# Hybrid decoder step: prompt scores in three rounded products, a sign-carrying search, and the rotary swap by transfers

## The chip, the cores and the metric

The kernel runs on one core of one Trainium2 chip. The metric is the device time in microseconds of that core; a kernel's time is the median of several executions, and one further execution is taken with the hardware profiler. TensorE multiplies matrices, VectorE (DVE), ScalarE (ACT) and GpSimd (POOL) work on rows, SyncE (SP) here only issues DMAs. They run side by side and meet at semaphores.

## The reference, cut to what matters

Two transformer layers for a prompt of 1024 tokens and 32 sample tokens (8 sequences of 4), model width 1024. Layer 0 is sparse attention, layer 1 a short convolution; both are followed by a SwiGLU. The change is in layer 0:

```
p = h @ w_in                              # 2120 columns: q (16 heads x 64), k, v (4 heads), indexer q, k, weights
q, k, qi, ki = partial_rope(...)          # the first 16 of 64 dims of a head are rotated: x1*c - x2*s, x2*c + x1*s
sc  = sum_h relu(qi_h . ki) * wi_h        # indexer score of each (query, key), -inf where not causal
sel = top_k(sc, 256)                      # 256 keys per prompt query
out = softmax(q . k over sel) @ v
```

The kernel does not gather keys. For each tile of 128 queries it finds the threshold above which 256 scores lie, makes a mask from it, and adds the mask to dense scores. Ties go to the first keys, as in the reference.

## The kernel before

All activations lie with features on partitions and tokens along the row: 1056 columns, taken as 3 chunks of 352. Numbers are float32. Large products are made of three matmuls of rounded parts (L590, `product`): high x high, high x low, low x high, where the high part is the value rounded to the short format (ScalarE copies it) and the low part the remainder (GpSimd or VectorE subtracts). Such a matmul takes one pass; a plain float32 matmul is recorded as two instructions.

**Projections.** 17 column tiles of `w_in` in the order of `ORDER`, each in 3 chunks; one (tile, chunk) is an item. Tiles 0 to 4 (indexer, `pe_proj_a`, L930) come before the indexer, tiles 5 to 16 (k, v, q, `pe_proj_b`, L961) after it. ScalarE evicts an item from PSUM (`act_evac_rope`, L997). For the rotation, TensorE multiplies the evicted item by a constant 128 x 128 matrix `rotm` that swaps rows 0-7 with 8-15 of each head (`pe_rot`, L844). In the first part VectorE multiplies the result with the sines and adds the cosine part (`dve_rope`, L1085); in the second ScalarE evicts it to `pafB` (`act_rot`, L1008) and GpSimd multiplies and adds (`pool_fin`, L1109). The cosine part is GpSimd's (`pool_cos`, L1102). Rotated q goes through DRAM (`q_scr`) and comes back to `hhi` after the last product (`sp_att`, L1389). Between items TensorE also multiplies chunks of the conditioning matrix (`pe_chunks`, L851), whose weights SyncE loads.

**Indexer and search.** `pe_index`, `act_index` and `dve_index` make the scores of query tiles 2 to 7 in `s_all`. Then VectorE searches the thresholds bit by bit (`dve_select`, L1578) while TensorE works on tiles 5 to 16: 32 rounds, in each of which VectorE counts the scores of tiles 2 to 5 and the samples against a candidate, and ScalarE those of tiles 7 and 6 (`act_count`, L893), at places in its own order that `count_halves` (L101) writes down in advance. The scores of a tile are first multiplied by a sign, so that all thresholds are positive, and multiplied back when the masks are made.

**Attention.** 64 pairs (`NPAIR`), pair n being query tile n // 8 and head step n % 8, two heads at once in two groups of 64 partitions. The order of a pair on each engine, with four slots of probabilities and scores three pairs ahead (`pe_att`, L1915):

- TensorE: turns (transposes) of the first head's probabilities (L1866, L1871), values of pair n-1 (L1884), turns of the second head's, scores of pair n+3 (`pe_scores`, L1838; plain float32, L1855), chunks of the conditioning matrix.
- VectorE: a step or two of the masks (`dve_masks_at`, L1713, pairs 0 to 27), evictions of turns, the inverse of the sums of pair n+1 (L1949), the output of pair n-1, mask and minimum of pair n+3 (L1942).
- ScalarE: eviction of each head's turn (L1993), exponential of pair n+2 (L1986), output of pair n-1 (L1998); then splits of output weights in pairs 49, 52, 55 and 58.
- GpSimd: normalisation of pair n by the inverse (L2023), which TensorE's turn of pair n waits for; then the low parts of output weights in pairs 50, 53, 56 and 59.

Query tiles 0 and 1 have fewer than 256 keys and take the causal mask alone.

Of the kernel before, what the change touches and what calls it, by code (L numbers as in the profile page):

```python
# [350 lines left out]
def program(nc, x_prompt, x_sample, c_prompt, c_sample, cache_k, cache_v, cache_kidx, state_conv, page_table,  # L351
            ada_w, ada_b, norm1_g, norm2_g, final_g, attn_w_in, attn_w_out, conv_w_in, conv_k, conv_w_out,
            ffn_w_gu, ffn_w_down, k_ident, k_rot, k_cos, k_sin, k_causal, k_causal_s, k_bitf, k_biti,
# [10 lines left out]
    with ExitStack() as ctx:  # L364
# [22 lines left out]
        (rotm,) = place(616 + 540, ("rotm", [P, P], F32))  # L387
# [94 lines left out]
        def wide(i):  # L482
# [15 lines left out]
        evac, rot_mm, ts_rdy, pm_rdy, qc_rdy, fin_rdy = (sem(x) for x in (  # L498
            "evac", "rot_mm", "ts_rdy", "pm_rdy", "qc_rdy", "fin_rdy"))
# [125 lines left out]
        def sp_start(sp):  # L625
# [22 lines left out]
            sp.dma_start(rotm[:], k_rot).then_inc(const_loaded, 16)  # L648
# [31 lines left out]
        def dve_start(dve):  # L680
            dve.memset(ones[:], 1.0)
            dve.memset(bv[:, 0:9], 1.0).then_inc(f_st, 1)
# [158 lines left out]
        def rot_bank(r):  # L841
            return bank[(3, 5)[r % 2] if r < 15 else (3, 4)[r % 2]]
# [50 lines left out]
        def act_count(act, half):  # L893

            for h in range(64):
# [34 lines left out]
        def pe_proj_a(pe):  # L930
            pe.wait_ge(const_loaded, 64)
            pe.wait_ge(ada_read, G0)
            for p in range(5):
                for n in range(NCH):
# [3 lines left out]
                    for r in {0: (), 1: (), 2: (0,), 3: (1, 2)}.get(3 * p + n, (3 * p + n - 1,)):  # L938
                        pe_rot(pe, r)
# [10 lines left out]
            pe_rot(pe, 14)  # L950
# [10 lines left out]
        def pe_proj_b(pe):  # L961
            pe.wait_ge(relu_rdy, 8 * len(TILES))
            for n in range(NCH):
                pe_tile(pe, 5, n)
                if n:
                    pe_rot(pe, R_AT[5] + n - 1)
                pe_chunks(pe, ITEM_AT[5] + n)
            pe.wait_ge(up_lo, 8)
            for tt in range(9):
# [7 lines left out]
                if tt == 0:  # L977
                    pe_rot(pe, R_AT[5] + 2)
                pe_chunks(pe, ITEM_AT[6] + tt)
            for p in (8, 9):  # L980
                for n in range(NCH):
                    pe_tile(pe, p, n)
                    if p == 9 or n:
                        pe_rot(pe, R_AT[p] + n - 1)
                    pe_chunks(pe, ITEM_AT[p] + n)
            pe.wait_ge(fin_rdy, R_AT[9])
            for p in range(10, 17):
                for n in range(NCH):
                    pe_tile(pe, p, n)
                    pe_rot(pe, R_AT[p] + n - 1)  # L990
# [3 lines left out]
            pe_rot(pe, R_AT[16] + 2)  # L994
            pe_ada_turned(pe, SG_W - 1)

        def act_evac_rope(act, p, n, dst):  # L997
# [3 lines left out]
            after(act, rot_mm, r - 1)  # L1001
# [6 lines left out]
        def act_rot(act, r):  # L1008

            act.wait_ge(rot_mm, r + 1)  # L1010
            after(act, fin_rdy, r - 1)
            act.activation(pafB[:, r % 2, :], rot_bank(r)[:, 0:CH], ACT.Copy).then_inc(ts_rdy, 1)

        def act_proj_a(act):
            for p in range(5):
                for n in range(NCH):
                    if p or n:
                        act_evac_rope(act, p, n, psgA)
                proj_hi(act, p + WR)
# [8 lines left out]
        def act_proj_b(act):  # L1028
            for n in range(NCH):
                act_evac_rope(act, 5, n, psgB)  # L1030
                act_count(act, 2 * (ITEM_AT[5] + n))
                if n:
                    act_rot(act, R_AT[5] + n - 1)
                act_chunks(act, ITEM_AT[5] + n)
            for tt in range(9):
# [5 lines left out]
                if tt == 0:  # L1041
                    act_rot(act, R_AT[5] + 2)
                    proj_hi(act, 9)
                act_chunks(act, ITEM_AT[6] + tt)
            for p in (8, 9):
                for n in range(NCH):
                    act_evac_rope(act, p, n, psgB)
                    act_count(act, 2 * (ITEM_AT[p] + n))
                    if p == 9 or n:
                        act_rot(act, R_AT[p] + n - 1)  # L1050
# [4 lines left out]
            for p in range(10, 17):  # L1055
                for n in range(NCH):
                    act_evac_rope(act, p, n, psgB)
                    act_count(act, 2 * (ITEM_AT[p] + n))
                    act_rot(act, R_AT[p] + n - 1)
# [5 lines left out]
            act_rot(act, R_AT[16] + 2)  # L1065
# [19 lines left out]
        def dve_rope(dve, r):  # L1085
# [3 lines left out]
            dve.wait_ge(rot_mm, r + 1)  # L1089
            after(dve, fin_rdy, r - 1)  # L1090
            dve.tensor_tensor(pafA[0:rows, r % 2, :], rot_bank(r)[0:rows, 0:CH], ropeS[0:rows, chunk(n)], ALU.mult)\
# [17 lines left out]
        def pool_fin(pool, r):  # L1109

            p, n = (5, r - 15) if r < 18 else (8 + (r - 18) // 3, r % 3)
            pool.wait_ge(ts_rdy, r + 1)
            pool.tensor_tensor(pafB[:, r % 2, :], pafB[:, r % 2, :], ropeS[:, chunk(n)], ALU.mult).then_inc(pm_rdy, 1)
            pool.wait_ge(pm_rdy, r - 14)
# [12 lines left out]
        def pool_proj_b(pool):  # L1127
            for p in (5,) + tuple(range(8, 17)):
# [2489 lines left out]
```

## Time and profile before

| | |
|---|---|
| time, median of 3 runs | 2634.79 us (2630.44 to 2640.76) |
| profiled execution | 2635.32 us, span of the profile 2633.5 us |
| TensorE, matmul | 2512.0 us busy, 95% |
| VectorE, ScalarE, GpSimd | 1771.3, 1101.9, 1287.4 us busy |
| granted TensorE clock | 0.983 of full speed, mean |

The span is the time from the first to the last instruction; the few microseconds around it belong to the execution's own time. Busy times are sums over instructions. PE stands for TensorE's matmuls, PEld for its weight loads, and SPq for SyncE's queue. L12 is line 12 of the kernel. A busy TensorE is not one at its peak, since matmuls are pipelined.

### The profile page before, as it was taken

The numbers are of one execution on the slowest core, as the hardware profiler recorded it, in microseconds if no ns is written. First come the engines' busy times: TensorE is split into PE (matmuls) and PEld (weight loads), VectorE is DVE, ScalarE is ACT, GpSimd is POOL, SyncE is SP. The second block draws the span as 40 slices with busy tenths as digits, with TensorE's granted clock in tenths as the row PEclk, the third lists the DMA queues.
The fourth block names the chain that finished last, engine by engine and source line by source line (L and its number), as shares of the span: only waits on it lengthen the run. The fifth ranks groups of instructions, "written<-read, shape, count | busy, mean of one in ns | idle before, by whom it ended". The sixth has DMA issues, their size and how long they took to land.

```text
span 2633.5 us, 51699 instructions
## 1 busy us (share of the span) xinstructions
PE 2512.0 (95%) x20164; PEld 2312.3 (88%) x20164; DVE 1771.3 (67%) x3137; ACT 1101.9 (42%) x2061; POOL 1287.4 (49%) x967
## 2 busy tenths in 40 slices
PE   6979999999998999999999989999989999999999
PEld 4848874677798999999999989999989999999999
DVE  6388888665347756656567687767785665656775
ACT  5155656775235444344212343332454444442223
POOL 3404652344134656566544545545455656654454
PEclk7999999999999999999999999999999999999999
DMA  9205557201433435344894333328334534469731
GB/s 322 78 21 153 177 207 255 70 2 68 129 113 101 146 124 164 117 155 139 328 349 167 117 98 106 107 82 328 117 98 131 164 117 155 139 207 366 278 131 70
DMA packets 316390, 408.00 MB, mean 155 GB/s; under 512 B 40816, under 2 KB 227032, under 8 KB 313338
## 3 DMA queue, kind: packets, MB, share of 16 engines
q1 hardware_dynamic: 316154, 404.75, 45.9%
q8 instruction: 161, 2.64, 0.4%
q14 instruction: 75, 0.61, 0.1%
HBM read 284.85 MB, written 119.85 MB: 154 GB/s over the span
## 4 chain that ended last, share of the span: by engine, by line
PE 70%; DVE 11%; DMA 6%; issue 5%; POOL 4%; ACT 2%; SPq 2%; ACTq 0%; DVEq 0%; POOLq 0%
PE PS L595 10%; PE PS L2492 9%; PE PS L2494 9%; PE PS L2493 9%; PE PS L2553 5%; PE PS L2555 5%; PE PS L2556 5%; PE PS L1855 3%; PE PS L1884 2%; PE PS L1866 2%; POOL ring L2864 2%; DMA t_scratch<-stage 2%; DMA a_scratch<-stage 1%; POOL stage L2877 1%; DVE s_all L1552 1%
## 5 line engine op out<-in xcount | busy, mean ns | idle before, releaser
L2492 PE MATMUL PS<-th,ring 128*128 128x264 f32 x2800 | 800.2, 286 | 19.9 <-DVE y L3007 8.2
L2494 PE MATMUL PS<-th,ring 128*128 128x264 f32 x2800 | 796.8, 285 | 0.0
L2493 PE MATMUL PS<-th,ring 128*128 128x264 f32 x2800 | 795.9, 284 | 0.0
L2492 PEld LDWEIGHTS PS<-th,ring 128*128 128x128 f32 x2800 | 527.8, 189 | 26.8 <-issue 26.1
L2493 PEld LDWEIGHTS PS<-th,ring 128*128 128x128 f32 x2800 | 528.0, 189 | 0.0
L2494 PEld LDWEIGHTS PS<-th,ring 128*128 128x128 f32 x2800 | 527.9, 189 | 0.0
L2864 POOL TENSOR_TENSOR ring<-wraw,ring 128x512 fp32r<-128x512 f32 x232 | 340.3, 1469 | 368.1 <-ACT ring L2648 367.8
L2864 POOL TENSOR_TENSOR ring<-sums,ring 128x512 fp32r<-128x512 f32 x216 | 322.2, 1493 | 276.3 <-ACT ring L2648 276.3
L2553 PE MATMUL PS<-th,ring 128*128 128x264 f32 x1232 | 354.8, 288 | 14.3 <-DVE zs L3196 6.7
L2555 PE MATMUL PS<-th,ring 128*128 128x264 f32 x1232 | 352.9, 286 | 0.0
L2556 PE MATMUL PS<-th,ring 128*128 128x264 f32 x1232 | 352.5, 286 | 0.0
L2648 ACT ACTIVATE ring<-wraw 128x512 fp32r<-128x512 f32 x340 | 211.8, 626 | 299.2 <-PE PS L2556 168.2
L3193 DVE SCALAR_TENSOR_TENSOR y<-PS,mod,y 128x528 f32<-128x528 f32 x308 | 235.0, 766 | 141.2 <-PE PS L2556 128.0
L3007 DVE TENSOR_TENSOR y<-y,PS 128x528 f32<-128x528 f32 x150 | 104.9, 699 | 293.8 <-PE PS L2494 293.6
L2648 ACT ACTIVATE ring<-sums 128x512 fp32r<-128x512 f32 x216 | 136.1, 631 | 353.2 <-PE PS L2494 173.3
L2553 PEld LDWEIGHTS PS<-th,ring 128*128 128x128 f32 x1232 | 234.4, 190 | 16.1 <-issue 11.7
L2556 PEld LDWEIGHTS PS<-th,ring 128*128 128x128 f32 x1232 | 234.7, 191 | 0.0
L2555 PEld LDWEIGHTS PS<-th,ring 128*128 128x128 f32 x1232 | 234.6, 190 | 0.0
L2877 POOL TENSOR_TENSOR stage<-y,stage 128x528 fp32r<-128x528 f32 x110 | 179.2, 1629 | 77.3 <-ACT stage L2668 77.3
L595 PE MATMUL PS<-hhi,uhi 128*128 128x352 f32 (+1 forms) x552 | 189.0, 342 | 14.5 <-DVE hlo L1267 7.3
L2696 ACT ACTIVATE y<-PS 128x528 f32<-128x528 f32 x173 | 105.1, 607 | 186.4 <-PE PS L2494 185.3
L595 PE MATMUL PS<-hhi,ulo 128*128 128x352 f32 (+1 forms) x552 | 180.8, 328 | 0.0
(393 smaller groups left out, 5164.4 us busy)
## 6 DMA issues: line engine op xcount, KB each, us to landing
t_scratch<-stage SPq DMA_DIRECT2D x154, 528.0 KB, 3.3
th<-t_scratch SPq DMA_DIRECT2D x77, 1056.0 KB, 8.7
wraw<-in_ffn_w_gu_dram SPq DMA_DIRECT2D x96, 512.0 KB, 5.2
wraw<-in_ada_w_dram SPq DMA_DIRECT2D x80, 512.0 KB, 4.8
wraw<-in_ffn_w_down_dram SPq DMA_DIRECT2D x80, 256.0 KB, 5.9
wraw<-in_conv_w_in_dram SPq DMA_DIRECT2D x28, 512.0 KB, 5.3
y<-y_scratch SPq DMA_DIRECT2D x12, 1056.0 KB, 8.9
y_scratch<-y SPq DMA_DIRECT2D x6, 2112.0 KB, 7.9
```

What stands on the lines that cost most here:

```text
L595: last = pe.matmul(out, w(kt), x(kt), start=(n == 0), stop=(n == 3 * count - 1))
L2492: pe.matmul(out, hi, x[:, TH, k, :], start=(k == 0 and i in (1, 2, 5)), stop=False, skip_group_check=True)
L2493: pe.matmul(out, hi, x[:, TL, k, :], start=False, stop=False, skip_group_check=True)
L2494: last = pe.matmul(out, lo, x[:, TH, k, :], start=False, stop=(k == 3), skip_group_check=True)
L2553: pe.matmul(out, hi, x[:, TH, 2 * k + s, :], start=(k == 0 and i in (1, 2, 5)), stop=False, skip_group_check=True)
L2555: pe.matmul(out, hi, x[:, TL, 2 * k + s, :], start=False, stop=False, skip_group_check=True)
L2556: last = pe.matmul(out, lo, x[:, TH, 2 * k + s, :], start=False, stop=(k == 1), skip_group_check=True)
L2648: act.activation(slot_of(p)[:, RH, :], split_source(p), ACT.Copy).then_inc(w_hi, 1)
L2696: act.activation(out, result(r, it.groups), ACT.Silu if it.kind == "g" and pos == 6 else ACT.Copy).then_inc(rd_a, 1)
L2864: pool.tensor_tensor(w[:, RL, :], split_source(p), w[:, RH, :].bitcast(F32), ALU.subtract).then_inc(w_lop, 1)
L2877: pool.tensor_tensor(lo.rearrange("p (s n) -> p s n", s=2), token_part(v, i), hi.rearrange("p (s n) -> p s n", s=2), ALU.subtract).then_in ...
L3193: ins = dve.scalar_tensor_tensor(out=out, in0=result(r, BOTH), scalar=gate_of(f, m)[:, 0:1], in1=out, op0=ALU.mult, op1=ALU.add)
```

## The change

1. **Rotation.** `rotm`, `pe_rot` and `act_rot` are gone. ScalarE issues DMAs that copy rows 8-15 of each head onto rows 0-7 of a second buffer and the other way round (`act_swap`, from the evicted item, four transfers of 8 rows by 352 columns, two for the three items of tile 0). The rest of that buffer is zeroed once. VectorE and GpSimd wait for the transfers.
2. **Search.** Scores are no longer multiplied by a sign. The candidate carries it, and bits are set with exclusive or; 31 rounds in place of 32; the five small steps of a round stand behind all counts. `count_halves` spaces ScalarE's counts anew.
3. **Masks** lose their multiplication by the sign.
4. **Scores of tiles 2 to 7.** q comes back to `hlo`. ScalarE writes rounded halves of q and k (`act_q_hi`), GpSimd the remainders (`pool_q_lo`), k in pairs 0 to 4, q in pairs 5 to 27, and TensorE makes three matmuls for each of the old ones. Tile 4 is cut in 320 + 320 columns. The halves of k hold two of the four slots of split weights to the last scores.
5. **Output weights** are split in pairs 50, 61, 62 and 63, on ScalarE and GpSimd in the same pair.

```diff
-    return [next(s for s, t in enumerate(at) if t >= 24 + 4.9 * h) for h in range(64)]
+    return [next(s for s, t in enumerate(at) if t >= 14 + 5.2 * h) for h in range(62)]
...
-        def pe_rot(pe, r):
-            rows = P if r >= 3 else 64
-            pe.wait_ge(evac, rope_m(r) + 1)
-            after(pe, ts_rdy, r - 1)
-            src = (psgA if r < 15 else psgB)[0:rows, r % 2, :]
-            pe.matmul(rot_bank(r)[0:rows, 0:CH], rotm[0:rows, 0:rows], src, start=True, stop=True).then_inc(rot_mm, 1)
+        def swap_done(eng, r):
+
+            if r >= 0:
+                eng.wait_ge(swapped[r % 2], sum(32 if x < 3 else 64 for x in range(r % 2, r + 1, 2)))
+
+        def act_swap(act, r):
+
+            act.wait_ge(evac, rope_m(r) + 1)
+            after(act, fin_rdy, r - 1)
+            if r in (15, 16):
+                act.wait_ge(pm_rdy, 1)
+            src, dst = (psgA, pafA) if r < 15 else (psgB, pafB)
+            for head in (0,) if r < 3 else (0, 64):
+                for o in (head, head + 8):
+                    of = 2 * head + 8 - o
+                    act.dma_start(dst[o:o + 8, r % 2, :], src[of:of + 8, r % 2, :]).then_inc(swapped[r % 2], 16)
...
                     act_evac_rope(act, p, n, psgB)
                     act_count(act, 2 * (ITEM_AT[p] + n))
-                    act_rot(act, R_AT[p] + n - 1)
+                    act_swap(act, R_AT[p] + n)
...
-            dve.tensor_tensor(pafA[0:rows, r % 2, :], rot_bank(r)[0:rows, 0:CH], ropeS[0:rows, chunk(n)], ALU.mult)\
+            swap_done(dve, r)
+            dve.tensor_tensor(pafA[0:rows, r % 2, :], pafA[0:rows, r % 2, :], ropeS[0:rows, chunk(n)], ALU.mult)\
...
-            return xn[:, t, at] if t == KT - 1 else hhi[:, t, at].bitcast(F32)
+            return xn[:, t, at] if t == KT - 1 else hlo[:, t, at].bitcast(F32)
+
+        SPLIT0 = 2
+        K_AT, KL_AT = {0: 0, 1: 1}, {1: (0, 0), 2: (0, 1), 3: (1, 0), 4: (1, 1)}
+        Q_AT = {5: (2, 0), 7: (2, 1), 9: (3, 0), 11: (3, 1)} | {13 + 2 * x: (4 + x // 2, x % 2) for x in range(8)}
...
+        def act_q_hi(act, n):
+
+            if n in K_AT:
+                a = K_AT[n]
+                act.wait_ge(up_mm, UP_END[14 + a])
+                act.wait_ge(fin_rdy, 21)
+                act.activation(k_part(uhi, a), kT[:, a, 0:SEQ], ACT.Copy).then_inc(q_hi, 1)
+            if n in Q_AT:
...
+                ts = slice(4, KT - 1) if h else slice(0, 4)
+                ins = act.activation(hhi[:, ts, at], hlo[:, ts, at].bitcast(F32), ACT.Copy)
+                if h:
+                    act.wait_ge(fin_rdy, 45)
+                    ins = act.activation(hlo[:, KT - 1, at], xn[:, KT - 1, at], ACT.Copy)
+                ins.then_inc(q_hi, 1)
+
+        def pool_q_lo(pool, n):
...
+            if n in Q_AT:
+                i, h = Q_AT[n]
+                at = slice(P * i, P * i + P)
+                pool.wait_ge(q_hi, Q0 + 2 + 2 * (i - SPLIT0) + h + 1)
+                ts = slice(4, KT - 1) if h else slice(0, 4)
+                ins = pool.tensor_tensor(hlo[:, ts, at], hlo[:, ts, at].bitcast(F32), hhi[:, ts, at].bitcast(F32), ALU.subtract)
+                if h:
+                    ins = pool.tensor_tensor(hhi[:, KT - 1, at], xn[:, KT - 1, at], hlo[:, KT - 1, at].bitcast(F32), ALU.subtract)
+                ins.then_inc(q_lo, 1)
...
+            with dve.Fori(0, ROUNDS) as i:
+                dve.wait_ge(sel, i * 6 + base)
+                count(2, None, ALU.is_ge)
+                dve.wait_ge(cand_rdy, i + 1)
+                signal(count(6, None, ALU.is_lt))
+                count(3, None, ALU.is_ge)
+                count(4, None, ALU.is_ge)
+                signal(count(5, None, ALU.is_ge))
+                dve.wait_ge(sel, i * 6 + (base + 1))
                 dve.wait_ge(sign_cnt, i * NA + NA)
...
+                signal(dve.tensor_tensor(v(lt, 0, 3), v(cnt, 0, 3), v(kk, 0, 3), ALU.is_gt))
...
             if step == 0:
-                link(dve, dve.tensor_scalar(s, s, bv[0:rows, BS + 3 * E + j:BS + 3 * E + j + 1], None, ALU.mult))
                 link(dve, dve.tensor_scalar(A, s, t, 0.0, ALU.is_gt, ALU.add, accum_out=n))
...
+            if i < SPLIT0:
...
+            if t % 4 == 0:
+                pe.wait_ge(q_lo, Q0 + 4 + 2 * (i - SPLIT0) + t // 4 + 1)
+            (hi, lo), a = q_parts(i, t), t // 4
+            cs = pieces(i)
             for j, c in enumerate(cs):
-                for g in range(2):
-                    last = pe.matmul(wide(2 * g)[:, c], q_of(i, t)[64 * g:64 * g + 64],
-                                     kT[64 * g:64 * g + 64, t // 4, c], start=True, stop=True)
-                    if j == len(cs) - 1:
-                        last.then_inc(s_mm, 1)
+                for x, (q, w) in enumerate(((hi, uhi), (lo, uhi), (hi, ulo))):
+                    for g in range(2):
+                        last = pe.matmul(score_of(i, g, j, c), q[64 * g:64 * g + 64], k_part(w, a)[64 * g:64 * g + 64, c],
+                                         start=(x == 0), stop=(x == 2))
+                        if j == len(cs) - 1 and x == 2:
+                            last.then_inc(s_mm, 1)
...
                 act_pair_chunks(act, n)
-                if n in (49, 52, 55, 58):
-                    split_hi(act, "out", (n - 49) // 3, MM0["out"])
+                act_q_hi(act, n)
+                if n in OUT_AT:
+                    if n > 60:
+                        act.wait_ge(s_mm, 2 * NPAIR)
+                    split_hi(act, "out", OUT_AT.index(n), MM0["out"])
...
                     pool.tensor_scalar(p, p, bv[:, at:at + 1], 1.0, ALU.mult, ALU.mult).then_inc(p_nrm, 1)
-                if n in (50, 53, 56, 59):
-                    split_lo(pool, "out", (n - 50) // 3)
+                pool_q_lo(pool, n)
+                if n in OUT_AT:
+                    split_lo(pool, "out", OUT_AT.index(n))
```

## Rows read from the trace of the kernel before

**Rows 1.** The page, part 1: busy us of each engine (share of span), instructions.
```profile
PE 2512.0 (95%) x20164; PEld 2312.3 (88%) x20164; DVE 1771.3 (67%) x3137; ACT 1101.9 (42%) x2061; POOL 1287.4 (49%) x967
```

**Rows 2.** Windows by stage: stretch, length, busy us, clock, DMA share, GB/s.
```profile
65.00:134.00 69.00, 65.97 (x372) 58.53 (x372) 27.70 (x57) 12.40 (x23) 33.24 (x28) 0.95 0.29 79
...
185.00:382.00 197.00, 194.29 (x1342) 162.34 (x1343) 175.86 (x636) 111.91 (x223) 101.33 (x95) 0.98 0.51 157
...
382.00:482.00 100.00, 90.35 (x829) 45.78 (x828) 80.20 (x248) 62.16 (x215) 32.04 (x62) 0.95 0.78 254
...
386.00:397.00 11.00, 9.15 (x58) 3.84 (x58) 5.31 (x24) 3.86 (x20) 2.96 (x8) 0.53 0.94 350
```

**Rows 3.** Chain of waits from 262 us: start, us, engine, line.
```profile
264.28 4.01 PE PS L595 x24
...
268.30 0.59 PE PS L849 x2
```

**Rows 4.** The same view, 382 to 652 us, shares by line.
```profile
by line: PE PS L1855 24.7%; PE PS L1884 24.0%; PE PS L1866 20.8%; DMA wraw<-in_ada_w_dram 8.2%; PE PS L1871 5.8%; PE PS L1897 4.6%; issue 3.1%; DVE mscr L1699 2.3%; DVE PbS L1942 1.3%; DVE mscr L1697 0.8%; POOL PbS L2023 0.8%; DVE s_all L16
```

**Rows 5.** Groups by line, ScalarE, 185-382 us: busy, mean ns, idle before.
```profile
L900 ACT ACTIVATE junkA<-s_all,bv 128x1024 bf16<-128x1024 f32 x64 | 69.8, 1091 | 41.0 <-DVE bv L1640 41.0
...
L1005 ACT ACTIVATE psgB<-PS 128x352 f32<-128x352 f32 x30 | 13.8, 460 | 35.9 <-PE PS L595 35.9
```

**Rows 6.** Timeline, SyncE's queue: start us, us of issuing, line.
```profile
4.58 0.30 SPq L635 DMA_DIRECT2D vst<-in_c_prompt_dram  x1
...
4.92 0.66 SPq L636 DMA_DIRECT2D vst<-in_c_sample_dram  x1
```

**Rows 7.** DMA issues: count, KB each, median us to landing.
```profile
q_scratch<-qst_ SPq DMA_DIRECT2D x21, 176.0 KB, 2.5
```

**Rows 8.** Timeline, pair 5: start us, us, engine, line, idle before.
```profile
404.13 0.30 PE L1866 MATMUL PS<-ident,PbS 128*128 128x128 f32 x1
...
404.64 0.39 ACT L1986 ACTIVATE PbS<-PbS,bv 128x128 f32<-128x128 f32 x1
...
405.53 0.72 POOL L2023 TENSOR_SCALAR PbS<-PbS,bv 128x128 f32<-128x128 f32 x2 [3.14 <-DVE bv L1949]
...
406.00 0.33 PE L1866 MATMUL PS<-ident,PbS 128*128 128x128 f32 x1
```

**Rows 9.** Timeline, pair 27.
```profile
479.59 0.66 PE L1866 MATMUL PS<-ident,PbS 128*128 128x128 f32 x4
...
480.78 0.71 ACT L1986 ACTIVATE PbS<-PbS,bv 128x512 f32<-128x512 f32 x1
...
481.54 0.66 PE L1866 MATMUL PS<-ident,PbS 128*128 128x128 f32 x4
```

**Rows 10.** Timeline, pair 50.
```profile
576.65 0.66 PE L1866 MATMUL PS<-ident,Pb 128*128 128x128 f32 x4
...
579.27 0.66 PE L1866 MATMUL PS<-ident,Pb 128*128 128x128 f32 x4
```

**Rows 11.** Timeline, pair 61.
```profile
637.97 0.66 PE L1866 MATMUL PS<-ident,Pb 128*128 128x128 f32 x4
...
638.30 2.21 POOL L2023 TENSOR_SCALAR Pb<-Pb,bv 128x1024 f32<-128x1024 f32 x2 [3.65 <-DVE bv L1949]
...
639.16 1.14 ACT L1986 ACTIVATE Pb<-Pb,bv 128x1024 f32<-128x1024 f32 x1
...
639.47 0.66 PE L1866 MATMUL PS<-ident,Pb 128*128 128x128 f32 x4 [0.41 <-POOL Pb L2023]
```

**Rows 12.** The page, part 5: remainder and rounded half, 512 columns.
```profile
L2864 POOL TENSOR_TENSOR ring<-wraw,ring 128x512 fp32r<-128x512 f32 x232 | 340.3, 1469 | 368.1 <-ACT ring L2648 367.8
...
L2648 ACT ACTIVATE ring<-wraw 128x512 fp32r<-128x512 f32 x340 | 211.8, 626 | 299.2 <-PE PS L2556 168.2
```

**Rows 13.** Lines 580 and 587, the same of 1024 columns: ns min/median/max.
```profile
L580 ACT ACTIVATE uhi<-wraw x12: 1039/1053/1062, 573.7 to 782.6; 128x1024 fp32r<-128x1024 f32 x12
...
L587 POOL TENSOR_TENSOR ulo<-wraw,uhi x12: 2362/2373/2422, 574.8 to 783.7; 128x1024 fp32r<-128x1024 f32 x12
```

More of the change, by code:

```diff
@@ L681, in dve_start @@
             dve.memset(ones[:], 1.0)
+            dve.memset(pafA[:], 0.0)
             dve.memset(bv[:, 0:9], 1.0).then_inc(f_st, 1)
@@ L893, in act_count @@
         def act_count(act, half):
-            for h in range(64):
+            for h in range(62):
                 if COUNT_AT[h] == half:
@@ L1592, in dve_select, with v, vi @@
-            one = lambda r, j: v(r, j, j + 1)
-            ka = bank[5][:, 432:432 + NA]
-            groups = ((0, NA), (NA, E))
-            def count(j, threshold):
+            cnt, lt, kk, low, th, cand, inc = range(7)
+            held = {lt: 384, kk: 400, inc: 416}
+            tiny = 1.1754943508222875e-38
+            def v(r, a=0, b=E):
+                return bank[5][:, held[r] + a:held[r] + b] if r in held else bv[:, BS + E * r + a:BS + E * r + b]
+            def vi(r, a=0, b=E):
+                return v(r, a, b).bitcast(I32)
@@ L1598, in count, with one @@
+            def one(r, j):
+                return v(r, COL[j], COL[j] + 1)
+            def count(j, threshold, op):
                 s, rows, L, _ = entries[j]
                 at = threshold if isinstance(threshold, float) else one(cand, j)[0:rows]
-                return dve.tensor_scalar(junk(j, rows, L), s, at, 0.0, ALU.is_ge, ALU.add,
-                                         accum_out=one(cnt, j)[0:rows])
+                return dve.tensor_scalar(junk(j, rows, L), s, at, 0.0, op, ALU.add, accum_out=one(cnt, j)[0:rows])
@@ L1603, in dve_select, with signal @@
+            def signal(ins):
+                ins.then_inc(sel, 1)
             dve.wait_ge(smp_rdy, 1)
             dve.wait_ge(score_rdy, 8 * len(TILES))
-            link(dve, dve.memset(bv[:, BS:BS + 7 * E], 0.0))
+            link(dve, dve.memset(v(cnt), 0.0))
             for j in range(E):
-                ins = count(j, 0.0)
+                ins = count(j, 0.0, ALU.is_ge)
+            for j in range(NA):
+                dve.memset(one(kk, j), float(entries[j][2] - 2 * entries[j][3]))
+            dve.memset(one(kk, E - 1), float(entries[E - 1][2] - entries[E - 1][3]))
@@ L1608, in dve_select @@
             link(dve, ins)
[L1609 to L1610 removed]
+            for a, b, k in ((0, 2, KP), (2, 3, KS), (3, E, KP)):
+                dve.tensor_scalar(v(th, a, b), v(cnt, a, b), float(k), 2.0, ALU.is_ge, ALU.mult)
+                ins = dve.tensor_scalar(v(cand, a, b), v(cnt, a, b), float(k), -1.9999998807907104, ALU.is_lt, ALU.mult)
             link(dve, ins)
[L1613 to L1615 removed]
@@ L1616, in dve_select @@
-            link(dve, ins)
-            for j, (s, rows, L, k) in enumerate(entries):
-                if j < NA:
-                    dve.tensor_scalar(ka[:, j:j + 1], one(kk, j), -2.0, float(L), ALU.mult, ALU.add)
-                dve.tensor_scalar(s, s, one(sig, j)[0:rows], None, ALU.mult)
-            ins = dve.memset(v(cand), 2.0)
+            ins = dve.tensor_tensor(v(cand), v(cand), v(th), ALU.add)
             link(dve, ins)
@@ new lines, in dve_select @@
+            nsel[0] += 6 * ROUNDS
+            dve.wait_ge(sel, nsel[0])
+            dve.wait_ge(cand_rdy, ROUNDS + 1)
+            dve.scalar_tensor_tensor(out=v(inc, 0, NA), in0=v(cand, 0, NA), scalar=tiny, in1=v(cand, 0, NA),
+                                     op0=ALU.is_ge, op1=ALU.mult)
+            link(dve, dve.tensor_scalar(v(lt, 0, NA), v(cand, 0, NA), 0.0, -tiny, ALU.is_lt, ALU.mult))
+            link(dve, dve.tensor_tensor(v(low, 0, NA), v(cand, 0, NA), v(lt, 0, NA), ALU.min))
+            link(dve, dve.tensor_tensor(v(th, 0, NA), v(inc, 0, NA), v(low, 0, NA), ALU.add))
@@ L1825, in program @@
         LA = NSLOT - 1
+        OUT_AT = (50, 61, 62, 63)
         def mask_of(i):
@@ L3568, in _constants @@
         S[o:o + 8], S[o + 8:o + 16] = -sin, sin
-        for d in range(8):
-            R[o + 8 + d, o + d] = R[o + d, o + 8 + d] = 1.0
     q, x = np.arange(P)[:, None], np.arange(SEQ)[None, :] - (SEQ - P)
```

172 lines of the change are left out of this document (70 added, 102 removed).

## The prediction

> **What bounds the kernel now.** I read the page first: TensorE is busy for 95% of the span [rows 1], so time leaves this kernel mostly where TensorE gets less to do or waits less. The windows by stage then say where the change falls [rows 2]: projections up to the indexer (65 to 134 us), the indexer, projections beside the search (185 to 382), attention pairs (382 to 652). Everything after 652 us, three quarters of the span, keeps its code; it only starts earlier or later. In both projection stretches TensorE is busy for nearly all of the time (65.97 of 69 and 194.29 of 197 us). The chain of waits there is nothing but its lines: a product of 24 matmuls of 352 columns in 4.01 us, then two passes of the rotation matmul, L849, in 0.59 us [rows 3]. In the attention stretch the chain of waits is scores (L1855), values (L1884) and turns (L1866) of TensorE, 70% together, with 8.2% of transfers [rows 4]. The last view is the timeline of single pairs, where I followed who frees whom: TensorE turns the probabilities, ScalarE evicts and exponentiates, GpSimd normalises the next pair, TensorE turns that one.
>
> **The rotation as transfers.** Removed: 45 matmuls of 0.59 us, 15 before the indexer and 30 after it [rows 3]. They lie on the chain, so 8.8 and 17.7 us of TensorE go. Added on ScalarE's queue are four transfers of 8 rows for each of them (two for the first three), 174 in all. Issuing is not shown for ScalarE. SyncE's small ones took 0.30 and 0.66 us [rows 6]; I take 0.33, so 1.3 us for a swap of four, as the 8-row one is the nearest. Zero is the lower end, where issuing runs beside an activation already handed over. ScalarE's load for an item of the second stretch is then: eviction 0.46 us; counts, 64 of 1.09 us with a read behind them over 39 items, some 2.1 us [rows 5]; weight splits, 8 of 1.05 us [rows 13], turned keys and the like some 0.5 together, an estimate; swaps 1.3; the eviction of the rotated rows goes. That is 4.4 us against TensorE's item of 5.2 - 0.6 = 4.6 us. It just fits; ScalarE waits 41.0 us for the search and 35.9 us for TensorE there now [rows 5], and that is the cover. With 0.66 us an issue it is 5.7 us an item and the cover is gone (a rival below). Landing: 176 KB take 2.5 us from issue [rows 7]; I take 2.5 for the small ones, bounds 1 and 6. A swap has one whole item before its buffer is wanted, so this costs nothing, except at two ends. Before the indexer the last swap takes 1.3 + 2.5 us where the matmul took 0.59; about half of the difference lies beside VectorE's additions for the item before, so +1.5. Before attention TensorE's third pair waits for the last rotated rows behind the same chain, in a stretch where DMA is at its limit (share 0.94 [rows 2]): +3. Sum: 8.8 - 1.5 = -7 before the indexer; -16 beside the search (17.7 less 10% for hold-ups by the shared order of evictions and counts); +3 at the start of attention. Together -20 us, bounds -27 and 0.
>
> The nearest row is of 176 KB and 128 partitions, and shows only that a transfer is not free of a fixed part. By the Trainium skill (DMA: Bandwidth & Descriptors, Rules for kernel authors) many small transfers should be joined, since below 64 KB one pays mostly overhead; no row here has 11 KB in one transfer. The Trainium skill gives 2.0 us as the fixed part of a transfer (same page, Anatomy of one DMA, measured there on GpSimd's path); with 2.0 in place of 2.5 us of landing the sum would be the same within a microsecond.
>
> **The search with signs carried.** One round less, one multiplication of each score tile less in front, two chains of three small steps made into one. ScalarE waits 41.0 us for the search [rows 5] and TensorE, busy for 194.29 of 197 us, waits for neither [rows 2]: the rounds run at TensorE's pace. With less to do in each and one fewer, I take it that they can follow the shorter item too, and cost them at nothing; the cover is TensorE's 4.6 us item. Without it each round would add its excess 31 times, up to the whole 16 us of the stretch. The masks lose one instruction of seven. They stand on the chain with L1699 and L1697, 3.1% of 270 us [rows 4]; I count nothing, bound -1.
>
> **Scores in three products.** The chain holds L1855 for 24.7% of 270 us, 66.7 us [rows 4], for 36,864 key columns in all pairs, 1.85 us per 1024. Now 1024 columns are six matmuls of 512 for each of two row groups. By [rows 3] a rounded matmul of 352 columns takes 0.167 us, so one of 512 at most 0.243, and six 1.46, if the two row groups run beside each other as they do in the four-pass form. That saves 0.39 us per 1024, over the 33,792 columns of tiles 2 to 7 12.9 us. Pairs in which TensorE waits anyway (below) give nothing back: -10, bounds -15 and 0. That the groups don't overlap is a rival.
>
> **The splits, and who waits for them.** This is the step I find dear. ScalarE makes the rounded half of q at the *end* of its work for pair n (`act_q_hi`), and GpSimd takes the remainder after the normalisation of the same pair n (`pool_q_lo`). GpSimd executes in order, so the normalisation of pair n+1, for which TensorE's next turn waits, stands behind a wait for ScalarE's end of pair n and the subtraction. Count from the second turn of pair n. Pair 5 [rows 8]: turn at 404.13, last exponential over at 405.03 (+0.90); rounded half 0.63, remainder 1.47 for 512 columns [rows 12]; first half of a normalisation 0.36. That makes +3.4 with a wait or two; the next turn now comes at +1.87. Price 1.6 us. Pair 27 [rows 9]: exponential and its read over at +1.90, rounded half and remainder in two pieces each 0.8 and 1.6, half a normalisation 0.7: +5.0, now +1.95. Price 3.0. There are 12 such pairs, every second from 5 to 27; between these ends, less at three of them where a transfer is late already, I read 22 us. Even pairs, where VectorE's masks and transfers hold TensorE a little now, give 2 back: +20, bounds +10 and +28. The splits of k are one pair or more apart and hold nobody.
>
> The output weights' splits have the same form now (`OUT_AT`: both engines in the same pair), where before GpSimd came one pair later. Pair 61 [rows 11]: exponential over at 640.30 + the read, +2.4 from the turn at 637.97; rounded half 1.05 and remainder 2.37 [rows 13], half a normalisation 1.1: +6.9, now +1.5. Price 5.4. Pair 62 has no exponential any more: 1.3 + 1.05 + 2.37 + 1.1 = +5.8 against some 1.4: 4.4. Pair 50 [rows 10]: 2.3 + 1.05 + 2.37 + 1.0 = +6.7 against +2.62: 4.1. The one of pair 63 is followed by no turn. Sum +14, bounds +10 and +16. TensorE idles for 4 to 5 us there. Its granted clock fell to 0.53 (the lower level, 1.2 GHz, for nearly all of it) in 386 to 397 us, after a stretch with short bursts [rows 2]; I add 2 us, bounds 0 and 8.
>
> **Sum.** -20 (swaps) + 0 (search) - 10 (scores) + 20 + 14 (waits for splits) + 2 (clock) = +6. The profiled execution took 2635.3 us (span 2633.5), half a microsecond above the median of 2634.8: forecast **2641 us**.
>
> **Rivals.**
> 1. *The splits are hidden* (2607 us). GpSimd is busy for a third of the attention stretch [rows 2], and three pairs of slots stand between scores and turn. If the wait for ScalarE cost GpSimd only its idle time, the terms +20, +14 and +2 go and 2635 - 20 - 10 = 2605 to 2609 remains. For it: GpSimd idles 3.1 to 3.7 us before its normalisations [rows 8, 11]. Against it: it idles because VectorE's inverse is late, and the order of the code puts the whole of ScalarE's pair in front.
> 2. *ScalarE becomes the bound beside the search* (2661). From 0.45 us an issue upwards its item is 4.9 us or more, from 0.55 on no gain of the 16 is left, and the same evictions reach GpSimd late: 2641 + 16 + 4. For it: 0.66 in [rows 6]; against it: the 8-row transfer's 0.30, and issuing may run beside counts.
> 3. *The row groups of a rounded matmul don't run beside each other* (2684). Twice 1.46 us per 1024 columns against 1.85: +1.07 x 33 = +35 in place of -10, some of it in pairs that wait anyway. Nothing in the trace has this form; the four-pass form overlaps.
> 4. *The clock stays low through the pairs with splits* (2655): each pair of pairs then has 2 to 3 us of idle. For it: 0.53 in 386 to 397 us, at the start of attention; against it: 0.95 over the whole of 382 to 482 us, which has gaps of 1 to 2 us too [rows 2]. From 10 us at the lower level on it decides.
>
> **How the numbers follow.** A change below 0.5% (13 us) can't be told from none here. My forecast has 0.45 (of it 0.80 within 13 us, 0.15 beyond it slower, 0.05 faster); rival 1 0.25 (0.9 faster); rival 2 0.15 (0.8 slower); rival 3 0.07 (slower); rival 4 0.08 (0.65 slower). So faster 0.25, same 0.44, slower 0.31. The range 2606 to 2668 takes in rival 1 and rival 2 and leaves out rival 3; the likeliest case by itself has 2629 to 2655.
>
> **What would show it.** Each step has its place in the profile after: no L849 and items of 4.6 us beside the search; the start of attention some 20 us earlier; in every second pair from 5 to 27 an idle of TensorE of 1.5 to 3 us released by GpSimd's normalisation, and GpSimd waiting for `act_q_hi`; idles of 4 to 5 us at pairs 51, 62 and 63; scores of 1024 columns in 1.5 us. Wrong it would be if ScalarE's queue shows issues above 0.45 us and TensorE waits for evictions, if GpSimd's normalisations come as early as now, or if two score matmuls of different row groups stand one behind the other.

## The result, and the profile after

| | before | after |
|---|---|---|
| median, us | 2635.2 | 2679.9 (2679.3 to 2683.8) |
| ratio to before | 1 | 1.0177, 95% interval 1.0163 to 1.0191 |
| profiled execution: span, us | 2633.5 | 2678.3 |

Slower by 45 us (1.8%), outside the range 2606 to 2668. The median before is that of four executions, the three of the table further up and one more. The page's busy times hardly moved: TensorE is busy for 6 us less than in [rows 1], at a lower mean granted clock (0.967 against 0.983), so the loss is waiting and a slower clock.

```profile
PE 2505.6 (94%) x20234; PEld 2329.1 (87%) x20234; DVE 1764.1 (66%) x3001; ACT 1101.4 (41%) x2047; POOL 1313.5 (49%) x990
```

To find the place I read the start times of the same events in both traces and subtracted them ("lag": after minus before, us; period sums are from pair to pair).

| event | before | after | lag |
|---|---|---|---|
| last eviction of a projection before the indexer | 126.0 | 121.0 | -5.0 |
| first one behind the indexer | 192.6 | 191.4 | -1.2 |
| last one beside the search | 379.9 | 364.9 | -15.0 |
| first turn of attention | 387.6 | 377.2 | -10.4 |
| turn of pair 5 | 403.3 | 392.2 | -11.1 |
| turn of pair 29 | 484.8 | 516.5 | +31.7 |
| turn of pair 50 | 574.1 | 600.9 | +26.8 |
| turn of pair 52 | 584.5 | 617.7 | +33.2 |
| turn of pair 61 | 635.1 | 665.3 | +30.2 |
| turn of pair 63 | 643.8 | 686.4 | +42.6 |
| end | 2633.5 | 2678.3 | +44.8 |

Two jumps make the loss: pairs 5 to 28 (+42.8) and the four pairs 50, 51, 61 and 62 (+18.7). All the rest together is a gain of 16.7 us, though the lag also grows in two places ahead of attention: by 3.8 us across the indexer, and by 4.6 us between the last eviction beside the search and the first turn. Single executions differ there: in six kernels with the same projections, swaps and search (this one, `no_scores`, `q_lag`, `both_lag`, `spread_lag` and `padded`, below) it starts between 375.1 and 378.1 us.

Windows of the changed kernel, against [rows 2] (length, then busy us of PE, PEld, DVE, ACT, POOL, granted clock, DMA share, GB/s). Read the clock column: 0.82 where it was 0.95.

```profile
65.00:134.00 69.00, 58.97 (x348) 54.12 (x346) 36.16 (x59) 14.20 (x25) 33.61 (x28) 0.90 0.35 93
...
382.00:482.00 100.00, 78.31 (x656) 41.41 (x654) 61.71 (x175) 50.71 (x176) 39.84 (x60) 0.82 0.55 180
```

The same view with one window a pair, pairs 21 to 24. In the odd ones, where q is split, TensorE is busy for 3.3 of 6.7 us; in the even ones it is busy from end to end, but at half the clock (1.2 GHz at 0.50) for much or nearly all of it, and takes 5.4 and 6.4 us for what took 4.1 before.

```profile
468.90:475.58 6.68, 3.30 (x37) 1.89 (x33) 6.27 (x10) 3.13 (x9) 2.85 (x3) 1.00 0.73 236
475.58:481.02 5.44, 5.44 (x42) 3.46 (x43) 1.46 (x4) 2.66 (x7) 1.63 (x3) 0.69 0.01 2
481.02:486.97 5.95, 3.25 (x34) 1.85 (x32) 4.52 (x13) 3.21 (x10) 2.13 (x4) 0.91 0.65 211
486.97:493.40 6.43, 6.43 (x43) 3.93 (x43) 1.46 (x4) 2.88 (x7) 1.96 (x3) 0.55 0.18 50
```

The chain of waits through pair 25 (start, us, engine and line) shows what TensorE idles for. After a last turn at 495.07 it is ScalarE's eviction (L2037), its exponential with the read of its sum (L2030), its rounded half of q (L1406), GpSimd's remainder (L1425), GpSimd's normalisation (L2070), and only then the next turn (L1908) at 500.03: 4.4 us, one behind the other.

```profile
495.07 0.60 PE PS L1908 x4
495.68 0.02 issue
495.70 0.03 ACT PT L2037
...
496.19 0.81 ACT PbS L2030 x2
497.00 0.53 ACT hhi L1406
497.53 0.07 issue
497.60 1.27 POOL hlo L1425
498.87 1.12 POOL PbS L2070
499.99 0.04 issue
500.03 1.11 PE PS L1908 x4
```

Issues of the swap's transfers on ScalarE's queue in the stretch beside the search (count, ns min/median/max). The median is nearly twice the assumed 0.33 us. 52 of the 120 run in part beside an instruction that ScalarE had been handed before them, most often a count, so issuing does run beside other work: from the first to the last eviction of this stretch (191.4 to 364.9 us) ScalarE executes for 96.8 us and issues for 74.0, 27 of them at the same time, and has nothing to do for 30.

```profile
L855 ACTq DMA_DIRECT2D pafB<-psgB x120: 631/632/1205, 191.9 to 368.0; - x120
```

Timeline of TensorE in pair 41: the three products of a score tile. x2 is the two row groups. The products start 0.33, 0.24 and 0.22 us after one another for both groups together, where the prediction took 0.243 for one matmul of 512 columns, so the groups run beside each other.

```profile
559.22 0.50 PE L1897 MATMUL PS<-uhi,hhi 64*128 64x512 f32 x2
559.55 0.39 PE L1897 MATMUL PS<-uhi,hlo 64*128 64x512 f32 x2
559.79 0.39 PE L1897 MATMUL PS<-ulo,hhi 64*128 64x512 f32 x2
560.01 0.28 PE L1897 MATMUL PS<-uhi,hhi 64*128 64x256 f32 x2
```

### The profile page after: what moved, and what is told of

It is laid out like the page before. It is cut to its first block, busy times and chain, and to the rows that moved or that the text cites. A ratio compares the mean times of both kernels' runs of the same rounds, so it can differ in the third digit from the quotient of the medians.

```text
span 2678.3 us, 51888 instructions
## 1 busy us (share of the span) xinstructions
PE 2505.6 (94%) x20234; PEld 2329.1 (87%) x20234; DVE 1764.1 (66%) x3001; ACT 1101.4 (41%) x2047; POOL 1313.5 (49%) x990
## 4 chain that ended last, share of the span: by engine, by line
PE 65%; DVE 11%; issue 6%; POOL 6%; DMA 5%; ACT 4%; ACTq 2%; SPq 1%; DVEq 0%; POOLq 0%
PE PS L2540 9%; PE PS L2542 9%; PE PS L2541 9%; PE PS L2601 4%; PE PS L594 4%; PE PS L2603 4%; PE PS L2604 4%; PE PS L1926 3%; PE PS L1908 3%; PE PS L1897 2%; POOL ring L2912 2%; ACTq L855 1%; DMA a_scratch<-stage 1%; DVE s_all L1603 1%; PE PS L2562 1%
## 5 line engine op out<-in xcount | busy, mean ns | idle before, releaser
L594 PE MATMUL PS<-hhi,uhi 128*128 128x352 f32 (+1 forms) x552 | 187.3, 339 | 14.6 <-DVE hlo L1257 7.3
L594 PE MATMUL PS<-hhi,ulo 128*128 128x352 f32 (+1 forms) x552 | 180.9, 328 | 0.0
```

What stands on the lines that cost most here:

```text
L594: last = pe.matmul(out, w(kt), x(kt), start=(n == 0), stop=(n == 3 * count - 1))
```

## The experiments

All medians in us; each ratio is against the kernel before, run on the same chip beside it. "Turn n" is the start of the first turn of pair n in the profiled execution.

### The parts alone

Three kernels carry one part of the diff each, on the kernel before.

`scores_only` (products, `act_q_hi`, `pool_q_lo`, `OUT_AT`):

> The kernel before with the attention's part of the change alone: prompt scores in three products of rounded halves, with the rounding of keys, queries and output weights where the changed kernel has it; rotation by TensorE and the old search stay. Theory A (the loss is made inside the attention, by VectorE's and TensorE's wait for the halves): the first turn to the last took 256.2 us before and 309.2 us after, so this kernel shows nearly all of it, +50 to +56 us (about 2688 us), more than the whole change, because the transfers' gain is missing. Rival B (ScalarE's issues of transfers are what costs): this kernel is at most +25 us (2660 us).

Measured 2689.1 (four executions, 2679.9 to 2695.5), ratio 1.019 (1.0155 to 1.0224): +55. First to last turn 312.4 us against 256.2. Theory A; the attention's part alone costs more than the whole change.

`swap_only`:

> The kernel before with the rotary swap by transfers alone. Theory A: faster by about 10 us (2625 us), since the first turn of the attention came 10.4 us earlier in the changed kernel. Rival B: each issue holds ScalarE 0.63 us where 0.33 us was assumed, ScalarE then holds back the search and the projections, and the kernel is slower by 10 us or more (2645 us). Rival C: the earlier start came from the new search, and the swaps alone change nothing beyond 3 us.

Measured 2635.8, ratio 0.9999 (0.9988 to 1.001): nothing. A's 10 us are missing; the first turn came 3.7 us earlier (383.9), and pairs 0 to 4 took 18.3 us instead of 15.7. That was the clock: TensorE was busy for 17.9 of the 18.3 us, all of it at the lower level (granted clock 0.50 from 367 to 408 us), where before it is back at 1.00 from pair 3 on. Rival B fails too: ScalarE was not what held it. By line in 185 to 382 us (busy, mean ns, idle before, releaser), its counts waited 41.6 us for VectorE's search.

```profile
L906 ACT ACTIVATE junkA<-s_all,bv 128x1024 bf16<-128x1024 f32 x64 | 69.8, 1090 | 46.1 <-DVE bv L1630 41.6 <-issue 4.5
```

The chain of waits had been TensorE's products there [rows 3]. In `swap_only` it is the search on VectorE (L1590 to L1635) and the short gaps between its steps ("issue"); the products (L594) are down to 7.7%. From the first to the last eviction beside the search it took 182.8 us, 187.3 before and 173.6 to 176.8 where the new search is there too.

```profile
by line: issue 32.5%; DVE junkA L1590 10.6%; PE PS L594 7.7%; DVE junkC L1590 7.4%; ACTq L855 6.6%; DVE PS L1628 4.6%; ACT junkA L906 4.3%; DVE junkB L1590 4.2%; DMA wraw<-in_ada_w_dram 2.6%; DVE bv L1630 2.5%; DVE bv L1635 2.3%; DVE PS L16
```

`search_only`:

> The kernel before with the sign-carrying search alone (31 rounds instead of 32, one step less in each mask, other places for ScalarE's counts). Theory A: within 4 us of before (2631 to 2639 us), as the projections set the pace beside the search. Rival C: it brings the 10 us that the attention starts earlier (2625 us).

Measured 2635.5, ratio 1.0 (0.9986 to 1.0013). Theory A.

`no_scores` has both of these parts together:

> The changed kernel with the attention of before: swaps by transfers and the new search, plain scores. Theory A (swap alone and search alone gave nothing, since each time the other held the pace, and together they start the attention 10 us earlier): about 2625 us, 8 to 12 us faster than before. Rival E (the earlier start is lost again in the attention's first pairs, on the weight transfers that pace them): 2632 us or more. With the version that has both low halves later, its difference tells what the three products are worth without waits: 6 to 9 us by theory A.

Measured 2624.7, ratio 0.996 (0.9948 to 0.9973): 10.4 us faster (the profiled execution, 2634.7, is the slowest of six). Neither part is worth anything alone, and together they give 10: the new search lets VectorE follow the shorter item. Rival E is out.

### The wait

`q_lag`, one edit to the changed kernel:

```
-                pool_q_lo(pool, n)
+                if n:
+                    pool_q_lo(pool, n - 1)
```

> The changed kernel with one edit: GpSimd takes the low half of keys and queries one pair later, behind the normalising of the next pair, so that it finds ScalarE's rounding done; the same instructions, the same number. Theory A (the loss of pairs 5 to 28, 43 us, is GpSimd's wait behind ScalarE's rounding, and TensorE's clock that falls in the pair behind each such wait): most of the 43 us go, 30 to 40 us, to about 2643 us, and the granted clock between 392 and 516 us goes from about 0.8 to over 0.95. Rival D (GpSimd's 1.2 us for the low half itself, not the wait, is too long for a pair): at most 15 us go (2665 us or more).

Measured 2633.7, ratio 1.0002 (0.9985 to 1.0018): 46 us back, more than theory A said. Pairs 5 to 28 took 79.3 us (before 81.5, after 124.3) with the same instructions. The window from 382 to 482 us has the clock at its upper level (2.4 GHz) throughout, and GpSimd busy for 55 of 100 us:

```profile
382.00:482.00 100.00, 95.07 (x982) 56.67 (x971) 81.91 (x238) 77.34 (x246) 55.30 (x83) 1.00 0.67 216
```

Rival D is out: GpSimd has time for its remainders; what cost was that it waited for ScalarE's last work of the pair with a normalisation queued behind.

`both_lag` keeps that edit and does the same with the output weights:

```
-                if n in OUT_AT:
-                    split_lo(pool, "out", OUT_AT.index(n))
+                if n - 1 in OUT_AT:
+                    split_lo(pool, "out", OUT_AT.index(n - 1))
+            split_lo(pool, "out", 3)      # behind the loop
```

> The changed kernel with both low halves one pair later on GpSimd: those of keys and queries, as in the run before, and those of the four output weights (behind the normalising of pairs 51, 62, 63, the last behind pair 63). Theory A (what is left of the attention's loss is the same wait at pairs 50, 61 and 62): pairs 50 and 51 together and 61 and 62 together go from 15.8 and 20.6 us to about 10.5 and 11 us, so 12 to 16 us below the version with the queries alone, about 2619 us, faster than before. Rival D (GpSimd's 2.34 us for one output weight is itself too long for a pair of 4.4 us): at most 5 us (2629 us).

Measured 2617.5, ratio 0.9927 (0.9899 to 0.9954), faster than before. Pairs 50 and 51 took 9.87 us together (15.83 with the queries alone), 61 and 62 also 9.87 (20.58). Rival D is out here too. By the medians it is 7.2 us faster than `no_scores`, which is about what the three products are worth without waits (6 to 9 were expected; the two intervals overlap a little, from 0.9948 to 0.9954).

`spread_lag` is `both_lag` without its last line, and moves the rounding to pairs 50, 59, 61, 62:

```
-        OUT_AT = (50, 61, 62, 63)
+        OUT_AT = (50, 59, 61, 62)
-                    if n > 60:
-                        act.wait_ge(s_mm, 2 * NPAIR)
+                    if n > 58:
+                        act.wait_ge(s_mm, 2 * NPAIR if n > 60 else 120)
```

> Both low halves one pair later, and the output weights' rounding spread to pairs 50, 59, 61 and 62 (low halves in 51, 60, 62, 63), since the first weight's and the last one's slots hold no key halves. Theory A: pairs 61 and 62 together take 8.8 to 9.0 us instead of 9.9, so 1 us off, 2616 us; it stays 16 to 19 us faster than before. Rival H (the half in pair 60 now collides with the full work of that pair, or the product behind the attention doesn't depend on it at all): no gain, 2617 to 2620 us.

Measured 2615.1, ratio 0.9939 (0.9924 to 0.9954). The intervals of the two overlap and pairs 61 and 62 still took 9.87 us, so theory A's microsecond is not there. The chain in `both_lag` shows why: the rounded half made at the end of pair 61 (L579) is still late for GpSimd in pair 62 (L586). `spread_lag` has the same pieces in the same place, 0.95 us at 618.47 and 2.35 us at 619.50, for another weight.

```profile
622.96 1.23 ACT Pb L2030 x2
624.19 0.95 ACT uhi L579
625.14 0.07 issue
625.22 2.35 POOL ulo L586
627.57 1.11 POOL Pb L2070
```

### The clock

`padded` is the changed kernel with its waits kept and filled: TensorE turns the identity 14 times ahead of the waits of pairs 6, 8, ... 28.

```
+            if g == 0 and n in range(6, 30, 2):
+                after(pe, eva, turned(n, g) - 1)
+                for j in range(14):
+                    pe.transpose(bank[4][:, 0:P], ident[:], ident[:])
             pe.wait_ge(p_nrm, turned(n, g))
```

> The changed kernel with GpSimd's wait as it is, but TensorE turns the identity 14 times (about 2.1 us of idle time filled, into the bank that the next turning writes) ahead of each even pair from 6 to 28. Theory A (the even pairs are longer only because the clock falls behind the wait of the odd pair): the 16 us that the even pairs grew by shrink to less than 5 us and the even pairs run at a granted clock over 0.9; the odd pairs stay as they are; some 8 to 14 us faster than the changed kernel, about 2669 us. Rival F (even pairs wait on the halves too): no gain, or slower by what the turnings cost, 2680 us or more.

Measured 2658.5, ratio 1.0094 (1.0074 to 1.0114): 21 us faster than the changed kernel with more work in it, more than expected. In the profiled executions 17.8 us of it lie in pairs 5 to 28; the rest lies where the edit is not, 2.1 of it ahead of the first turn. Its pairs 21 and 22:

```profile
456.97:463.66 6.69, 4.99 (x51) 3.41 (x47) 6.24 (x13) 3.13 (x9) 2.86 (x3) 1.00 0.74 235
463.66:467.60 3.94, 3.94 (x43) 2.43 (x44) 1.47 (x4) 2.48 (x7) 1.63 (x3) 1.00 0.02 4
```

The odd pair is as long as in the changed kernel (6.69 us), the even one is 3.94 instead of 5.44. Sums over the twelve of each:

| us | before | after | padded | queries later |
|---|---|---|---|---|
| odd pairs 5 to 27 | 42.5 | 69.5 | 68.7 | 40.8 |
| even pairs 6 to 28 | 38.9 | 54.8 | 37.8 | 38.5 |

So of the loss in pairs 5 to 28, 27 us are waiting and 17 us are the clock (the even pairs would otherwise have got 1.1 us shorter). In ten of the twelve even pairs the clock fell close to the end of the wait, between 1.1 us before and 1.8 us behind it, and was low in the pair that followed. The other two even pairs, 8 and 14, ran at 1.00, and only they did not grow: 2.54 and 3.07 us, against 2.54 and 3.19 before. The Trainium skill has this for waits on DMA (TensorE: Matmul & The Clock Gate, HAM oscillation: a wait in every step makes each step start at the slow clock); the runs agree, with an engine as the one waited for.

### The price of a transfer's issue

`half_swap` leaves out the swap of the second head of each pair of heads (on `both_lag`), two issues instead of four:

> The version with both low halves later, with two transfers a swap instead of four (the second head of each pair is left unrotated: part of the computation left out). Theory A (an issue holds ScalarE 0.63 us, and this bounds the projections beside the search as much as its work does): 27 projections lose 1.3 us of ScalarE each, and the first turn comes 10 to 25 us earlier, about 2605 us. Rival G (products, the search on VectorE or GpSimd's rotation hold the pace, the issues only fill ScalarE's idle time): the first turn within 4 us, 2615 us or more.

Measured 2609.2, ratio 0.9904 (0.9883 to 0.9925), an interval that overlaps that of `both_lag`; first turn at 370.3 against 378.1. That is 8 us, or 5 to 8 against the six kernels with the same projections and four issues: between the two theories, and not where theory A put it. From the first to the last eviction beside the search it took 173.8 us, no less than the six with four issues (173.6 to 176.8). The gain lies at the ends: 67.3 us across the indexer (last eviction before it to first one behind it) against 68.5 to 70.9, and 10.4 us from the last eviction to the first turn against 12.1 to 12.8.

`split_swap` cuts each transfer into halves of the columns (on `both_lag`), eight issues:

```
-                    act.dma_start(dst[o:o + 8, r % 2, :], ...)
+                    for part in (slice(0, 176), slice(176, 352)):
+                        act.dma_start(dst[o:o + 8, r % 2, part], ...)
```

> The version with both low halves later, each of the four transfers of a swap cut into two of half the columns: eight issues of 0.63 us, 2.6 us more of ScalarE's time for each swap. Theory A (an issue is as dear for half the bytes, and ScalarE's issues share in setting the pace beside the search): 27 projections get longer by up to 2.6 us, the first turn comes 25 to 60 us later, at 403 us or more, and the kernel is slower than before (2645 to 2680 us). Rival G (ScalarE has idle time for them): the first turn at most 10 us later (2628 us or less).

Measured 2719.3, ratio 1.0322 (1.0305 to 1.0339): first turn at 477.0, 99 us later. Its issues still took 0.63 us each, at half the bytes; 174 more of them are 110 us of ScalarE, and 90% of that shows. A part of the 99 us is the clock, which was not separated: it was granted 0.90 over 185 to 382 us, against 0.96 in `both_lag`. The shares of the chain of waits in 230 to 350 us with two, four and eight issues:

```profile
by line: PE PS L594 80.0%; PE PS L868 11.3%; DMA wraw<-in_ada_w_dram 4.4%; PE PS L961 1.6%; SPq L806 0.8%; SPq L745 0.6%; PE PS L881 0.5%; ACT psgB L1000 0.4%; SPq L744 0.4%; issue 0.2%
```

```profile
by line: issue 21.0%; ACTq L855 19.7%; PE PS L594 15.3%; ACT junkA L906 14.7%; DVE junkA L1654 5.3%; DMA wraw<-in_ada_w_dram 4.4%; ACT psgB L1000 3.4%; DVE junkC L1654 2.2%; PE PS L868 2.0%; DVE PS L1691 1.3%; ACT ktok L1016 1.3%; ACT uhi L
```

```profile
by line: ACTq L856 39.0%; PE PS L594 16.7%; issue 15.5%; ACT junkA L907 11.7%; PE PS L869 3.3%; DMA wraw<-in_ada_w_dram 3.2%; ACT psgB L1001 2.2%; POOL ulo L833 2.0%; POOL pafB L1101 1.6%; ACT uhi L827 1.2%; POOL kT L1107 1.0%; ACT ktok L10
```

With two issues the products hold the pace; with four the chain of waits passes between TensorE, ScalarE and its issues, which costs at most 3 us by the times above, so ScalarE's queue is near balance; with eight ScalarE holds the pace (246.7 us beside the search). There theory A holds, and by more than it said.

`no_swap_both_lag` puts TensorE's rotation back:

> Rotation by TensorE as before, new search, three products with both low halves one pair later. Theory A (the swaps bring their 10 us once the new search lets VectorE keep pace): slower by 8 to 12 us than the version with the swaps, about 2627 us, first turn at 387 to 390 us. Rival I (the swaps are worth nothing here either): within 3 us of it, 2615 to 2621 us.

Measured 2627.0, ratio 0.9974 (0.9961 to 0.9987), first turn at 383.4. With the new search and the later halves in place the swaps are worth 9.5 us by the medians. The profiled executions alone show less, 5.3 us at the first turn and 4.9 at the end; they differ by several us from one execution of a kernel to the next. Rival I is out; the first turn came 4 us earlier than expected.

## Why the prediction was wrong

Measured 44.8 us of span against +6 forecast, 39 more. Of these 21 lie in pairs 5 to 28 (+42.8 against +20 and the clock's +2), 10 in the swaps, 5 in the output weights, and the rest in what the scores gave less and behind the last turn.

**The step that failed: the clock behind the waits for splits.** The waits were predicted as they are, line for line: exponentials, rounded half, remainder, half a normalisation, turn. The term for the clock, "I add 2 us, bounds 0 and 8", was mis-sized: it is 17 us in pairs 6 to 28, and some 5 more in pairs 51 and 62.
- *Even pairs.* The sum took +20 for pairs 5 to 28, by "Even pairs [...] give 2 back". They took 15.9 us more instead. `padded` shows that this is the clock.
- *Odd pairs.* Prices of 1.6 and 3.0 us were worked out for pairs 5 and 27; 2.1 and 2.9 were measured. Their mean over twelve pairs is 27.6 us, but the prediction took 22; the twelve make 27.0 (0.76 to 2.9 each).
- *The clock.* Rival 4 had it at 10 us and more, with a chance of 0.08. The argument against it, 0.95 over 382 to 482 us with gaps of 1 to 2 us in it [rows 2], read gaps shorter than the predicted waits would add (TensorE idled 3.4 us in pair 21 and 2.7 us in pair 23). The row that applied was the 0.53 of 386 to 397 us: in the 5.6 us before the first turn of the kernel before, from 382.00 to 387.61, TensorE was busy for 1.9.

**Output weights**: +14 predicted; 5.4, 4.4 and 4.1 us for pairs 61, 62 and 50. Measured +5.4, +6.9 and +4.1, and +2.2 in pair 51 behind it: 18.7. The waits of pairs 61 and 50 are right. What is over, 2.5 us in pair 62 and 2.2 in pair 51, is put down to the clock by its level there (0.65 and 0.64); no run fills these waits.

**Swaps**: -20 predicted, -10.4 at the first turn, with the new search (9.5 by `no_swap_both_lag`). The three parts:
- *Before the indexer*, -7 predicted, -1.2 measured at the first eviction behind it. This is the larger part of the miss. The prediction gave issues and landing a price only for the last swap, since "A swap has one whole item before its buffer is wanted, so this costs nothing, except at two ends". Landings and issues are half of the chain of waits there:

```profile
by line: DMA pafA<-psgA 24.9%; ACTq L855 24.0%; DVE pafA L1078 11.2%; POOL ulo L833 11.1%; DVE qiT L1085 6.3%; PE PS L594 5.8%; ACT psgA L1000 4.3%; issue 3.0%; DVE kw L1085 2.7%; ACT uhi L827 1.4%; POOL qcA L1093 1.4%; DVE kw L1087 1.1%; P
```

  Of the 5.0 us gained at the last eviction, 3.8 were lost on the way to the next one: the last swap's four issues (2.5 us), 1.86 us of landing and VectorE's multiplication behind them (2.72 us at 125.36) all stand on the chain. The clock was also at its lower level for 13.7 us from 124.1 on, for 3.4 us from 130.4 on before.
- *Beside the search*, -16 predicted, -13.8 measured from the first to the last eviction. The issue was taken as 0.33 us and is 0.63: [rows 6] had 0.30 and 0.66, and the 0.66 was the one to take. Yet rival 2 ("from 0.55 on no gain of the 16 is left") did not come true either: it counted a swap for every item, where 30 of 39 have one, and 27 of 74 us of issuing ran beside other work of ScalarE. `split_swap` shows where rival 2 would have been right.
- *At the start of attention*, +3 predicted, +4.6 measured.

**Search**: costed at nothing, on the assumption that its rounds "can follow the shorter item too". Alone it is worth nothing, as said; the old one could not have followed (`swap_only`), which the prediction did not see.

**Scores**: -10 predicted. In pairs 29 to 49 the changed kernel gained 4.8 us, in 52 to 60 3.0, and `both_lag` 0.9 in 5 to 28 and 0.5 in 50 and 51, where nothing waits: 9.2 by the traces, 7.2 by the medians of `both_lag` and `no_scores`. The size is right, and rival 3 (row groups one behind the other) is out by the timeline.

**Rival 1**, splits hidden, 2607 us with a chance of 0.25, is out for this kernel, but it is what `spread_lag` (2615) is nearly: it took one pair of lag.

Sum by what was measured at the profiled execution: -10.4 (swaps and search) - 0.7 (pairs 0 to 4) + 42.8 (pairs 5 to 28: waits 27.0, clock 17.0, less 1.1 by which the even pairs are shorter at the upper level) - 4.9 + 6.3 - 3.0 + 12.3 + 2.2 behind the last turn = +44.6, against 44.8 of span. The last 2.2 us were not looked into; behind the last turn the thirteen profiled executions differ by 8 us.

## What to carry to other kernels

When an engine makes one half of a value and another engine the other half, place the second at least one step of the pipeline later: here one line moved by one pair gave 46 us back, with the same work. When a wait is added to TensorE, price it twice: the wait, and the stretch behind it at half the clock; the stretch of the trace in which TensorE idles as much as it will now tells at which level it then runs. When a part shortens the engine that sets the pace, name who is next and its distance: two parts that are worth 0 each gave 10 us together.

## What was not expected of the hardware

- Issuing one transfer took ScalarE's queue 0.63 us, the same for 11 KB and for half of it; an instruction handed over before goes on meanwhile, the next one waits. The Trainium skill says that initiating a DMA is usually small relative to the DMA itself (DMA: Bandwidth & Descriptors, Issuing engines are not separate DMA queues); here four issues take 2.5 us, and the last has landed 1.85 us behind its issue, so it is not small. The longest landing on the chain of waits was 6.2 us (98.14 us in the changed kernel's trace).
- Filling an idle of TensorE with useless work (14 turns ahead of each of 12 pairs) made the kernel 21 us faster, 17.8 of it in the pairs concerned.
